# Squares of the first and the latent norms taken earlier, an index search with operands in PSUM, and latent attention's scores as one fp32 product over 128 rows a head

## The reference

```python
def first_block(x, mem, ...):
    h = rmsnorm(x, g_mix)                       # the first norm
    dq, dk, dv, dz, db, da, cq, ckv, kix, wix = split(h @ w_in)
    ...                                         # gated delta rule on dq, dk, dv
    cq = rmsnorm(cq, q_norm_g)
    q_idx = (cq @ w_qidx).reshape(b, s, 8, 64)
    k_idx = layernorm(kix, ...)
    rel   = relu(einsum('bqhd,bsd->bqhs', q_idx, k_idx))
    score = einsum('bqh,bqhs->bqs', w_idx, rel)      # masked to s <= q
    _, idx = top_k(score, 256)                       # keys of the sparse attention
    x = x + concat([o_dn, o_dsa]) @ w_out
    x = x + cross_attention(rmsnorm(x, g_xattn), rmsnorm(mem, g_mem)) @ w_xo
    hf = rmsnorm(x, g_ffn)
    x = x + (silu(hf @ w_gate) * (hf @ w_up)) @ w_down
    return rmsnorm(x, g_final)

def second_block(x, c, positions, ...):
    c_act = silu(c)
    for l in range(2):
        shift, scale, gate = split(c_act @ w_ada[l] + b_ada[l])
        h = rms_norm(x, norm_g[l]) * (1 + scale) + shift
        fq, fk, fv, ff, fg, q_lat, kv_lat, k_r, mg = split(h @ w_in[l])
        y_fox = fox_attention(fq, fk, fv, log_sigmoid(ff + b_f[l])) * silu(fg)   # 8 heads of 64
        q  = rms_norm(q_lat) @ w_uq[l]        # 8 heads of 64 (nope) + 32 (rope)
        kv = rms_norm(kv_lat) @ w_ukv[l]      # 8 heads of 64 (k_nope) + 64 (v)
        # scores of a head: q_nope . k_nope + rope(q_rope) . rope(k_r), one k_r for all heads
        y_mla = mla_attention(q_nope, rope(q_rope), k_nope, rope(k_r), v) * silu(mg)
        x = x + gate * (concat([y_fox, y_mla]) @ w_out[l])
    return rms_norm(x, final_g)
```

## Time and profile before

| | |
|---|---|
| median of 3 runs | 3858.12 us (3856.49 to 3861.15) |
| profiled execution | 3861.46 us |
| its span | 3859.7 us |
| mean granted TensorE clock | 0.94 |
| busy share of PE, DVE, ACT, POOL | 89%, 50%, 31%, 28% |
| instructions | 46542 |

### The profile page before, as it was taken

The page is one execution under the profiler, slowest core; times in us unless marked ns, Lnnn a source line. Parts: engine busy times, 40 slices in busy tenths (PEclk is TensorE's granted clock), DMA queues, the critical chain, the costliest instruction groups (busy, mean ns, idle before and its releaser), DMA issues. The chain is left out here.

```text
span 3859.7 us, 46542 instructions
## 1 busy us (share of the span) xinstructions
PE 3424.0 (89%) x18228; PEld 2653.2 (69%) x18228; DVE 1929.1 (50%) x3226; ACT 1181.4 (31%) x2186; POOL 1075.7 (28%) x576
## 2 busy tenths in 40 slices
PE   6698799589788997999999978999898889998988
PEld 5366566469677876787887857776566677775657
DVE  2599577755545434736454471233554412335543
ACT  3344355434313221000000030333543212334540
POOL 2123000045235524444343443220101332201112
PEclk9799899689899998999999989998999899998999
DMA  3111000000212213313132112110102211000011
GB/s 110 28 28 38 30 4 3 1 8 2 77 39 61 61 39 98 95 60 103 55 98 65 55 28 88 34 28 1 23 1 72 77 40 44 23 6 17 7 66 66
DMA packets 228791, 171.13 MB, mean 44 GB/s; under 512 B 42224, under 2 KB 215840, under 8 KB 227840
## 3 DMA queue, kind: packets, MB, share of 16 engines
q1 hardware_dynamic: 225440, 167.81, 14.3%
q10 hardware_dynamic: 3168, 0.81, 0.1%
HBM read 151.66 MB, written 16.93 MB: 44 GB/s over the span
## 5 line engine op out<-in xcount | busy, mean ns | idle before, releaser
L929 DVE TENSOR_TENSOR I-13633act_f<-I-13632act_g,I-13639p_u 128x512 f32<-128x512 f32 x44 | 28.3, 684 | 238.8 <-PE I-13639p_u L287 238.8
L1097 DVE SCALAR_TENSOR_TENSOR y_T<-y_T 128x1024 f32<-128x1024 f32 x48 | 136.5, 2894 | 11.9 <-DMA y_T<-in_w_ada 11.9
L915 ACT ACTIVATE I-13632act_g<-I-13638p_g 128x1024 f32<-128x1024 f32 x22 | 22.6, 1028 | 388.0 <-PE I-13638p_g L287 388.0
L1662 DVE TENSOR_TENSOR I-22669S<-I-22669S,c_causal 128x256 f32<-128x256 f32 x32 | 13.8, 432 | 226.2 <-PE I-22669S L1600 226.2
L1662 DVE TENSOR_TENSOR I-16300S<-I-16300S,c_causal 128x256 f32<-128x256 f32 x32 | 13.8, 432 | 215.6 <-PE I-16300S L1600 215.6
L283 PE MATMUL I-13638p_g<-hf_hi,I-13614w_hi 128*128 128x512 f32 x352 | 109.7, 393 | 5.0 <-POOL hf_lo L509 5.0
L283 PE MATMUL I-13639p_u<-hf_hi,I-13615w_hi 128*128 128x512 f32 x352 | 109.1, 391 | 1.9 <-POOL I-13617w_lo L269 1.9
L287 PE MATMUL I-13638p_g<-hf_hi,I-13616w_lo 128*128 128x512 f32 x352 | 109.3, 392 | 0.0
L285 PE MATMUL I-13638p_g<-hf_lo,I-13614w_hi 128*128 128x512 f32 x352 | 109.2, 392 | 0.0
L285 PE MATMUL I-13639p_u<-hf_lo,I-13615w_hi 128*128 128x512 f32 x352 | 109.1, 391 | 0.0
L287 PE MATMUL I-13639p_u<-hf_hi,I-13617w_lo 128*128 128x512 f32 x352 | 108.8, 390 | 0.0
(11 more groups left out here) (1382 smaller groups left out, 10269.7 us busy)
## 6 DMA issues: line engine op xcount, KB each, us to landing
y_T<-in_w_ada SPq DMA_DIRECT2D x48, 512.0 KB, 3.6
saved_x<-x_T SPq DMA_DIRECT2D x3, 4096.0 KB, 12.4
x_T<-saved_x SPq DMA_DIRECT2D x3, 4096.0 KB, 13.5
I-13612w_raw<-in_w_gate SPq DMA_DIRECT2D x22, 512.0 KB, 4.5
I-13613w_raw<-in_w_up SPq DMA_DIRECT2D x22, 512.0 KB, 4.0
I-13626d_raw<-in_w_down SPq DMA_DIRECT2D x11, 512.0 KB, 4.6
I-13627d_raw<-in_w_down SPq DMA_DIRECT2D x11, 512.0 KB, 4.7
I-942w_raw<-in_w_in SPq DMA_DIRECT2D x8, 512.0 KB, 3.8
```

Source lines behind the costliest of these rows:

```text
L915: nc.scalar.activation(act_g[:, :], flat(p_g), ACT.Silu).then_inc(gated, 1)
L929: nc.vector.tensor_tensor(act_f[:, cols], act_g[:, cols], p_u[:, h, :], ALU.mult).then_inc(product, 1)
L1097: self.nc.vector.scalar_tensor_tensor(out=self.raw[s], in0=self.raw[s], scalar=1.0, in1=self.c_row, op0=ALU.mult, op1=ALU.mult, accum_out= ...
L1662: self.nc.vector.tensor_tensor(diag, diag, tiled(self.mask, 2), ALU.add).then_inc(self.masked, 1)
```

## The change

- `load_stage`: ACT squares each row tile as it arrives, with the sum over the features as a by-product (one sum a token, `row_sums`), ahead of the copy of the turned tile. The first norm takes its sums from there.
- `index_stage`: `w_lo` is made ahead of the constants; three tiles are counted on ACT; `need`, `below` and `flips` are in PSUM; two keeps go into the last loop.
- `cross_stage`: POOL waits for the norm's diagonal before its first split.
- `ffn_stage`: silu of c runs on ACT behind the norm; of POOL's eight adds of gained squares DVE takes four; `ada.finish` comes ahead of the last pair's adds.
- `fox_stage`: squares of the latents in units 3, 4 and 6 of pair 2, add in 5, sums in 7 in place of its half block, which goes to unit 0 of pair 3; root there, spreads in units 1 to 4.
- `mla_stage`: each head has 128-row operands `q_of` and `k_of`: 64 rows nope and 64 rows rotary part, so a score is one product. A Q block is one head; ACT copies its nope rows and DVE then rotates its rotary rows. The key's rotary rows are copied once to each of four tiles.
- `BlockAhead.pool` splits in four pieces of 256 columns.

```diff
@@ load_stage @@
+                        act.wait_ge(row_in[s], 16 * (i + 1))
+                        wait(act, squared[s], i)
+                        nc.scalar.activation(unread[s][:, :], rows[s][:, :], ACT.Square, accum_out=row_sums[:, 2 * i + s:2 * i + s + 1]).then_inc(squared[s], 1)
                         act.wait_ge(turned[s], i + 1)
@@ InverseRoot @@
-        dve.wait_ge(self.summed, self.groups)
-        v.tensor_scalar(self.var[:, :], self.sums, self.scale, EPS, ALU.mult, ALU.add).then_inc(self.scaled, 1)
+        if self.row_sums is None:
+            dve.wait_ge(self.summed, self.groups)
+        v.tensor_scalar(self.var[:, :], self.sums if self.row_sums is None else self.row_sums[:, :], self.scale, EPS, ALU.mult, ALU.add).then_inc(self.scaled, 1)
@@ BlockAhead @@
-        self.nc.gpsimd.tensor_tensor(self.hi, self.raw[:, :], self.ones[:, 0:1].to_broadcast([P, KD * P]), ALU.mult).then_inc(self.rounded, 1)
+        PIECE = 2 * P
+        for n in range(KD * P // PIECE):
+            part = slice(n * PIECE, (n + 1) * PIECE)
+            self.nc.gpsimd.tensor_tensor(self.hi[:, part], self.raw[:, part], self.ones[:, 0:1].to_broadcast([P, PIECE]), ALU.mult).then_inc(self.rounded, 1)
+            pool.wait_ge(self.rounded, n + 1)
+            self.nc.gpsimd.tensor_tensor(self.lo[:, part], self.raw[:, part], self.hi[:, part].bitcast(F32), ALU.subtract)
@@ ffn_stage @@
+            if last_pair:
+                ada.finish(dve)
...
-                for n in range(KD):
+                for n in range(KD // 2):
                     pool.wait_ge(g_squared[n % 2], n // 2 + 1)
...
                 ada.act(act)
                 norm.act(act)
+                ada.act_row(act)
@@ fox_stage @@
-                    if i < LAST:
-                        m = filler(i, t)
+                    m = filled(i, t)
+                    if (i, t) == (NORM, NT - 1):
+                        latent_sums(pe)
+                    if m is not None:
                         pe.wait_ge(hb.out, m)
+                        if i == LAST:
+                            pe.wait_ge(l_var_set, 2)
                         hb.multiply(pe, m, KD, half_of(m), hi, lo)
-                    elif t == 2:
-                        latent_sums(pe)
-                    elif t >= 4:
-                        latent_spread(pe, t - 4)
+                    if i == LAST and 1 <= t <= len(PARTS):
+                        latent_spread(pe, t - 1)
@@ mla_stage @@
-        hb = HalfBlocks(st, nc, const, KQ, [2, 2, 6, 2] * PAIRS, slots=4)
+        hb = HalfBlocks(st, nc, const, KQ, [2, 4, 4, 2] * PAIRS, slots=4)
...
-            rows = lambda h: slice(h * DH, (h + 1) * DH)
-            return [(lambda h, t: ph.q[i % 2][rows(h), t * P:(t + 1) * P], lambda h, a, b: ph.k[i % 2][rows(h), a:b]),
-                    (lambda h, t: q_rope[i % 2][rows(h), t * P:(t + 1) * P], lambda h, a, b: key_rope[rows(h), a:b])]
+            return [(lambda h, t: q_of[i % 2][h][:, t * P:(t + 1) * P], lambda h, a, b: k_of[i % 2][h][:, a:b])]
...
+                    elif b == BK:
+                        wait(act, hb.out, m)
+                        for h in range(2):
+                            rows = nope_rows[h]
+                            last = nc.scalar.activation(k_of[i % 2][h][rows, part], half_of(m)[rows, :], ACT.Copy, scale=scale)
+                        last.then_inc(hb.out, 1)
+                    else:
+                        rows = nope_rows[b - BQ0]
+                        nc.scalar.activation(q_of[i % 2][b - BQ0][rows, part], half_of(m)[rows, :], ACT.Copy).then_inc(q_copied, 1)
+
+                def copy_key(s):
+                    for h in range(2):
+                        nc.scalar.activation(k_of[s][h][rope_rows[h], :], key_rope[rope_rows[h], :], ACT.Copy).then_inc(key_copied, 1)
...
+                    dve.wait_ge(q_copied, q_halves(m) + 1)
+                    wait(dve, hb.out, m)
+                    nc.vector.tensor_tensor(q_of[m // 8 % 2][b - BQ0][rows, part_of(m)], half_of(m)[rows, :], turns_T[rows, part_of(m)], ALU.mult).then_inc(hb.out, 1)
@@ index_stage @@
-    ON_ACT = [3, 5]
+    ON_ACT = [1, 3, 5]
...
+        beside = S[1][:, HALVES - 1, BANK - 3 * NS:]
+        need, below, flips = beside[:, 0:NS], beside[:, NS:2 * NS], beside[:, 2 * NS:3 * NS].bitcast(I32)
...
+                    if r in (1, 4) and done < NB:
+                        keep(done)
+                        done += 1
...
+                dve.wait_ge(w_rounded, 1)
+                v.tensor_tensor(qw[2], qw[0], qw[1].bitcast(F32), ALU.subtract).then_inc(w_split, 1)
                 for r, n in enumerate(width):
@@ cross_stage @@
             def _(pool):
+                pool.wait_ge(norm.ir.diag_ready, 1)
```

189 lines of the change are left out of this document (108 added, 81 removed).

## The result

The changed kernel takes 3795.97 us (median of 4 runs, 3793.48 to 3797.06) against 3859.64 for the kernel before (4 runs, 3856.49 to 3862.5): a ratio of 0.9834, 95% interval 0.9817 to 0.9851, 63.7 us faster. The prediction was 3783, with 3765 to 3813 as its range.

What follows compares the result with a forecast made beforehand. The prediction took TensorE, busy 89% of the span, to bound the kernel nearly everywhere. Terms A to H summed to -75.7 us, from 3861.46 to 3785.8 profiled, median 3782.4, stated as 3783; range 3765 to 3813.

Steps and rivals of the forecast that it cites:

- likeliest case: Whole kernel: all terms hold as priced, forecast 3783 us, its own range 3770 to 3792; chance 0.52.
- rival 3: mla_stage loops: every rotation less its slack and each key piece is paid, +8 us a layer, total 3796; chance 0.13.
- A: load_stage: squares of the first norm move into the load, so its root comes earlier; -10.5 us (-8 to -12).
- B: index_stage: earlier weight split, small operands in PSUM, third Sign, keeps in the last loop; TensorE's blocks bound it; -37 us.
- Rival 1: index_stage: PSUM operands relieve nothing, block cadence 12 us instead of 10.9, stage -24, total 3795; chance 0.15.
- C: cross_stage: POOL waits until the norm's diagonal is built, which comes 5.4 us earlier; -3 us (-5 to +2).
- D: Head of ffn_stage: the norm's root no longer waits behind silu and its DMA; -7.8 us.
- E: End of ffn_stage: four of POOL's eight adds go to VectorE and finish moves ahead; -1.4 us (0 to -2.5).
- F: fox_stage, twice: latents' squares and sums move to pair 2, a half block to pair 3; -10 us (-16 to +8).
- H: BlockAhead, twice: POOL's split in pieces shortens VectorE's wait; -4 us a layer, -8 in all (0 to -9.4).
- G: mla_stage scores, twice: one 128-row product a head saves switches but adds copies and rotations; +2 us in all (-6 to +10).
- rival 5: mla_stage loops: new gaps at the copies lower TensorE's clock again and again, 3910 us, slower by 52; chance 0.03.

## Why the prediction was right, and where it was off

The time lies in the range, and 13 us above the point. Of 75.7 predicted, 68.0 are in the profiled execution; the medians are 4 closer together, the profiled run of after being the fastest of its four and that of before one of the slower. 3796 lies outside the 3770 to 3792 that the likeliest case gave itself, and it is the number that rival 3 named. That is a coincidence: rival 3 puts the loss on all of the loops, but behind unit 2 the loop is as long as before within 0.2 us a layer (the block ahead whole in both), and the time went into the key copies and the start of the stage.

- **A** predicted -10.5, measured -11.0 (undone: 11.0). The load grew by under 3.
- **B** predicted -37, measured -38.1 (49.2 less 11.0). The end was computed as a chain of 10.9 us blocks, and TensorE is busy in 123.3 of the 127 us from 213 and in all of the 26 from 340. Its three causes, undone alone, cost 18.7 (operands in SBUF), 13.6 (keeps), and nothing (third Sign). The order of the weights' split gave 3.2 (distance at the first count 14.3 against 11.0). Rival 1, by which operands in PSUM relieve nothing, is refuted; what the prediction would have lost by it, 13, measured 18.7. The Trainium skill, SBUF — State Buffer, "SBUF: two separate sides", has a VectorE instruction with two SBUF inputs wait for the whole of GpSimd's; by that rule, the trace agrees, 768 ns with both inputs in SBUF and 169 ns with one.
- **C** predicted -3, measured -3.2. **D** -7.8, measured -8.0. **E** -1.4, measured -2.2.
- **F** predicted -10, measured -5.3 in each layer of this trace. Layer 1 holds in all traces; layer 0 gives between nothing and 5.3, so the term is -5 to -11, and that the profiled run fell on the good side is luck.
- **H** predicted -8, measured -4.0 a layer behind unit 0 on average: right in size. But the scaling still takes 2.34, where the prediction's sign was nothing over 2, and in the latent attention of before pieces gave only 1.0 and 2.2.
- **G** is the step that went wrong, by its size: -4.3 of switches and +5.4 of costs were to give +1 a layer, and without pieces and without the longer start it is +4.9 (221.3 from gate to gate, 216.4 before). The term is the copy of the second buffer's rotary key rows, "+1.7", measured +5.1 a layer over units 0 to 2, and 4.5 came back when it was moved alone. I counted the copies on ScalarE and not the gap that they make for TensorE, nor the low clock behind it, though the earlier trace rows had just shown me that a gap of this kind is followed by a low clock. That is rival 5's mechanism, once a layer and not again and again. Of the other steps of G, the columns cost the same, 1.13 and 1.02 as before; a filled pair, with the rotations behind the keeps and the switches gone, is 0.2 to 0.6 longer (its first unit 0.8), and the last pair, which has no rotations, 0.9 shorter. Behind unit 2 that is -0.2 a layer without pieces, where 3.3 of rotations less 4.3 of switches were put down; what each of the two came to was not separated.
- What no step foresaw is the start of mla_stage, 19.2 and 19.3 us from the gate before to unit 0's mask, 16.9 before: +2.3 a layer. One of SyncE's DMA issues takes 1.2 us there in layer 0 and 1.7 in layer 1 instead of 0.43 to 0.47, and the first weights land later, so that GpSimd begins to split them 5.2 to 5.3 behind the gate, where it was 3.8 to 3.9. The rows below are of the changed kernel and of the run with the load and the block ahead of before: SyncE's four issues, and, from some six microseconds around them, the median time from issue to landing of the first weights. The first has one 16 KB transfer of the queue that the profile calls `instruction` there, the second has none:

```profile
2668.27 2.72 SPq L1561 DMA_DIRECT2D I-19073w_raw<-in_w_uq  x4
q8 instruction: 1, 0.02, 1.2%
I-19072w_raw<-in_w_ukv SPq DMA_DIRECT2D x2, 32.0 KB, 2.6
...
2682.49 1.96 SPq L1552 DMA_DIRECT2D I-19109w_raw<-in_w_uq  x4
I-19108w_raw<-in_w_ukv SPq DMA_DIRECT2D x2, 32.0 KB, 1.7
```

The two go together in every trace. Of the 28 starts in the fourteen traces, 22 have such a transfer 0.9 to 1.7 us behind SyncE's first issue, one issue of 0.9 to 1.8 us, and the first split 4.9 to 5.6 behind the gate. The other six (both of the kernel before, both of the run named above, and layer 1 of the two runs with latent attention of before) have no transfer there, no issue over 0.5, and the first split at 3.8 to 3.9. The starts take 18.5 to 19.6 with it and 16.2 to 17.8 without. So the +2.3 goes with where this transfer falls. Which engine it serves, and which of the edits moves it there, stays open; sixteen more instructions of SyncE did not move it.

Together G, H and the start come to +5.0 and +1.8 in the two layers, from gate to gate, where -3 each was predicted: 12.8 us short, some 8 of it G and 4.6 the start. The parts A to F were 3.4 better than predicted (73.1 for 69.7), and some 2 more came in the stages between. That leaves the 7.7 between 75.7 and 68.0. So A to F made up a part of the two errors in latent attention.

## What to carry to other kernels

Before pricing a stage whose engines work beside each other, find the one chain that will bound it after the change, and compute the end by its steps; here blocks of 10.9 us gave the end to 1 us, while the third Sign, on an engine that was not to bound it, gave nothing. Put one-time copies where the copying engine already waits, ahead of the loop: 2.1 us cost 3.3 to 4.5 in the loop and nothing ahead of it. Keep one operand of a small VectorE instruction out of SBUF where GpSimd runs beside it (169 ns for 768).

## What was not expected of the hardware

- A gap of TensorE in dense work cost more than its length: with 3.06 us of waiting, units 0 to 2 became 5.1 longer, 4.5 of which went with the copies, the granted clock of the ten microseconds around it being 0.66.
- Products over 64 rows on the two halves paired up by themselves when the queue held them head by head; with a 2-row fp32r product between them they did not, and fox_stage's scores took twice as long (1.48 a head against 1.49 for two).
- A small VectorE instruction with one input can stand still too: L398, float to float in SBUF, took 2.20 beside GpSimd's split, while L2357, from float to integer, also in SBUF in the run with the three operands there, averaged 172 ns over 31.
- A 16 KB transfer of the instruction queue at the start of a stage goes with a DMA issue of SyncE of 0.9 to 1.8 us, where its neighbours take 0.43 to 0.47, and with a start that is 1.5 to 2.6 us longer in the changed kernel's latent attention.
